# Gate and up of two feed-forwards by Strassen's scheme, in rounds, with two of four weight sums by accumulating DMAs

## The reference

```python
def swiglu(x, w_gate, w_up, w_down):
    return (jax.nn.silu(x @ w_gate) * (x @ w_up)) @ w_down
...
        h = h + 0.5 * swiglu(rms_norm(h, ffn1_norm[l]), ffn1_w_gate[l], ffn1_w_up[l], ffn1_w_down[l])
        u = rms_norm(h, mix_norm[l])
        z = u @ w_in[l]
...
        merged = jax.nn.sigmoid(ga) * (ya @ w_branch_a[l]) + jax.nn.sigmoid(gb) * (yb @ w_branch_b[l])
        h = h + merged @ w_out[l]
        h = h + 0.5 * swiglu(rms_norm(h, ffn2_norm[l]), ffn2_w_gate[l], ffn2_w_up[l], ffn2_w_down[l])
    return rms_norm(h, final_norm)
```

## Time and profile before

| | us |
|---|---|
| runs of the kernel | 1712.38, 1714.38, 1716.47 |
| median | 1714.38 |
| profiled execution, span | 1712.4 |
| TensorE busy in it | 1690.3 |
| VectorE busy | 817.3 |
| ScalarE busy | 614.4 |
| GpSimd busy | 140.8 |

### The profile page before, as it was taken

How to read it: one execution, slowest core, us unless ns; L and a number is a source line. 1 busy time by engine, 2 the same in 40 slices (tenths; PEclk the granted TensorE clock), 3 DMA queues, 4 the chain that set the end, 5 groups by cost and what they waited for, 6 DMA issues and landing times.

```text
span 1712.4 us, 22979 instructions
## 1 busy us (share of the span) xinstructions
PE 1690.3 (99%) x8175; PEld 1369.3 (80%) x8175; DVE 817.3 (48%) x1277; ACT 614.4 (36%) x1066; POOL 140.8 (8%) x149
## 2 busy tenths in 40 slices
PE   7999999999999999999999999999999999999998
PEld 5777688888888887888888887777888888888888
DVE  4888755443333344444444325765555444444332
ACT  3565644222223233222222222655543322223222
POOL 0120210000001140000001131011001100000000
PEclk9999999999999999999999999999999999999999
DMA  9743134433342334333343346122233333333332
GB/s 326 244 130 112 43 93 123 147 107 92 95 116 85 101 103 130 98 98 98 97 119 97 92 133 117 50 63 70 77 95 99 94 93 96 98 98 111 102 95 73
DMA packets 298929, 184.60 MB, mean 108 GB/s; under 512 B 14555, under 2 KB 285335, under 8 KB 298855
## 3 DMA queue, kind: packets, MB, share of 16 engines
q1 hardware_dynamic: 294112, 169.89, 33.1%
q0 software_dynamic: 4400, 13.82, 3.4%
q10 hardware_dynamic: 360, 0.13, 0.0%
HBM read 180.67 MB, written 6.36 MB: 109 GB/s over the span
## 4 chain that ended last, share of the span: by engine, by line
PE 93%; DVE 3%; ACT 2%; DMA 1%; issue 1%; DVEq 0%; ACTq 0%; SPq 0%
PE psum L567 29%; PE psum L569 28%; PE psum L568 28%; PE psum L996 1%; PE psum L961 1%; PE psum L773 1%; PE psum L1016 1%; PE psum L733 1%; DMA w_raw<-in_ffn_w_gate 1%; PE psum L749 1%; DVE w_lo L1641 1%; DVE p L1794 0%; ACT p L1289 0%; PE psum L654 0%; DMA ident<-in_k_ident 0%
## 5 line engine op out<-in xcount | busy, mean ns | idle before, releaser
L567 PE MATMUL psum<-h_hi,w_hi 128*128 128x512 f32 x1480 | 586.4, 396 | 4.6 <-DVE w_lo L1641 2.8
L569 PE MATMUL psum<-h_hi,w_lo 128*128 128x512 f32 x1480 | 576.7, 390 | 0.0
L568 PE MATMUL psum<-h_lo,w_hi 128*128 128x512 f32 x1480 | 576.6, 390 | 0.0
L1641 DVE TENSOR_TENSOR w_lo<-w_raw,w_hi 128x1024 fp32r<-128x1024 f32 (+2 forms) x266 | 348.6, 1311 | 305.0 <-ACT w_hi L1229 301.2
L1229 ACT ACTIVATE w_hi<-w_raw 128x1024 fp32r<-128x1024 f32 (+2 forms) x266 | 288.2, 1084 | 165.0 <-PE psum L569 153.4
L567 PEld LDWEIGHTS psum<-h_hi,w_hi 128*128 128x128 f32 x1480 | 277.9, 188 | 85.3 <-issue 23.9
L569 PEld LDWEIGHTS psum<-h_hi,w_lo 128*128 128x128 f32 x1480 | 277.9, 188 | 59.3
L568 PEld LDWEIGHTS psum<-h_lo,w_hi 128*128 128x128 f32 x1480 | 278.1, 188 | 55.9 <-issue 1.0
L567 PE MATMUL psum<-hid_hi,w_hi 128*128 128x512 f32 (+1 forms) x550 | 209.6, 381 | 0.0
L569 PE MATMUL psum<-hid_hi,w_lo 128*128 128x512 f32 (+1 forms) x550 | 209.3, 381 | 0.0
L568 PE MATMUL psum<-hid_lo,w_hi 128*128 128x512 f32 (+1 forms) x550 | 209.3, 381 | 0.0
(11 more groups left out here) (266 smaller groups left out, 1383.5 us busy)
## 6 DMA issues: line engine op xcount, KB each, us to landing
w_raw<-in_w_in SPq DMA_DIRECT2D x50, 512.0 KB, 3.7
w_raw<-in_w_gate_up SPq DMA_DIRECT2D x44, 512.0 KB, 3.7
w_raw<-in_ffn_w_gate SPq DMA_DIRECT2D x44, 512.0 KB, 3.7
w_raw<-in_ffn_w_up SPq DMA_DIRECT2D x44, 512.0 KB, 3.6
w_raw<-in_ffn_w_down SPq DMA_DIRECT2D x32, 704.0 KB, 4.5
w_raw<-in_w_down SPq DMA_DIRECT2D x16, 704.0 KB, 4.5
sq<-in_w_ada SPq DMA_DIRECT2D x20, 512.0 KB, 4.9
ada_w<-in_w_ada SPq DMA_DIRECT2D x16, 512.0 KB, 10.9
```

The costliest lines, as they stand in the source:

```text
L567: pe.matmul(o, a_hi, b_hi, start=start, stop=False)
L568: pe.matmul(o, a_hi, b_lo, start=False, stop=False)
L569: return pe.matmul(o, a_lo, b_hi, start=False, stop=stop)
L1641: dve.tensor_tensor(w_lo[:, s % 2, 0:n], w_raw[:, s % 2, 0:n], w_hi[:, s % 2, 0:n].bitcast(F32), ALU.subtract).then_inc(w_ready, 1)
```

## The change

For gate and up of feed-forwards 1 and 2 the product of a 2 x 2 block matrix is done with 7 block products in place of 8 (Winograd's form of Strassen's scheme). The input is cut into token halves (256) and halves of K (512 channels); the weights into gate and up, and the same halves of K. A unit is 256 columns of gate and the same of up: two hidden tiles. 11 units make up a feed-forward.

- **Inputs.** 7 blocks, A11, A12, A22 and the combinations R1 to R4, each with 4 x 256 elements per partition, high (`hq_hi`) and low (`hq_lo`). VectorE makes the combinations per channel block in `combos` (L2359) as the down or output product before it is finished; for channel blocks 0 to 3 that is one subtraction and a split of 512 elements, for 4 to 7 three operations and a split of 1280.
- **Weights.** Raw blocks in 2 sets of 5 buffers: B11 and B21 are the gate's halves of K, B12 and B22 the up's. T1 = gate half 1 added to the B12 buffer, T3 = up half 2 added to a second copy of up half 1: both by GpSimd DMAs that accumulate at their destination (`add_weights`). T2 = T1 + B22 and T4 = T2 + B21 are additions of VectorE (L2187), in place, behind the split of what they overwrite. Split weights go through a ring of 4 slots (`ring_hi`, `ring_lo`; `high` on ScalarE, `lower` L2179 on VectorE), which also serves the down projections.
- **Products** of a unit, in TensorE's order (3 x 8 matmuls of 256 tokens each): B11 into bank Y; T1 into Z; T2 onto Y; half of B21 into X; T3 onto Y; the other half of B21; T4 onto Y; B22 onto Z. In between Y holds sums that others must read first: ScalarE copies them from PSUM (`s1` before the T2 product, `u2` before T3's, `u3` before T4's), and VectorE's `first_gate` (X + s1, L2276), `second_gate` (L2285), `first_up` (Z - u2, L2294) and `second_up` (Z - u3, L2268) make gate and up of both token halves.
- **Rounds.** Units 0 to 3, 4 to 6 and 7 to 10; behind each a partial down projection over its hidden tiles, added to the residual. All three feed-forwards have these rounds; feed-forward 0 keeps its plain gate and up products. The feed-forwards' loops are unrolled.
- **out2** and feed-forward 0's last round run over channel blocks in the order `PAIRED`: 0, 4, 1, 5, and so on.
- At the second mixer's entry its first slab's split now stands behind the last block's `h_hi` and squares.

The diff, cut to its core, indented less (`f_prod` counts finished products, `prod[...]` is a product's number in it):

```diff
+TQ = T // 2
+KQ = KD // 2
+KU = KF // 2
+ROUNDS = [(0, 4), (4, 7), (7, KU)]
+KR = 2 * max(b - a for a, b in ROUNDS)
+PAIRED = [0, 4, 1, 5, 2, 6, 3, 7]
...
+hq_hi = place("hq_hi", [P, 7, KQ, TQ], F32R, HQ_AT)
+hq_lo = place("hq_lo", [P, 7, KQ, TQ], F32R, OVER)
+A11, R3, A12, A22, R1, R2, R4 = range(7)
...
+        for n, name in enumerate(("B11", "B12", "B12+", "B22", "B21")):
+            load_at((name, f, u), set_, n)
+        for name in ("P1", "Q5", "P6", "P2a", "P7", "P2", "Q4", "Q3"):
+            finish_at((name, f, u))
+        for name, n, done_ in (("B11", 0, "P1"), ("T1", 1, "Q5"), ("T2", 1, "P6"), ("T3", 2, "P7"),
+                               ("B21", 4, "P2"), ("T4", 1, "Q4"), ("B22", 3, "Q3")):
+            split_at((name, f, u), slot_no % 4, (set_, n), (done_, f, u))
+            slot_no += 1
...
+            plan(("Y", f, u), 3 * (u % 2), (f_prod, prod["Q4", f, u]), (gate_set[1], m))
+            plan(("X", f, u), 3 * (u % 2) + 1, (f_prod, prod["P2", f, u]), (c11_set, m))
+            plan(("Z", f, u), 3 * (u % 2) + 2, (f_prod, prod["Q3", f, u]), (c12_set, m))
...
+    if f == 0 and r == 0:
+        plan(("mod", GT2 // KD), 4)
...
+        plan(("down", f, r, n), 6 + i % 2, (f_prod, prod["down", f, r, n]), read)
...
+def downs(f, r, between=None):
+    ks, order = range(2 * ROUNDS[r][0], 2 * ROUNDS[r][1]), downs_of(f, r)
+    down_part(f, r, order[0], ks[:-2], True)
+    down_part(f, r, order[1], ks[:-2])
+    down_part(f, r, order[0], ks[-2:], True)
+    down_part(f, r, order[1], ks[-2:])
+    if between is not None:
+        between()
...
+def product(bank_, item, q, f, u, tiles=(0, 1), first=False, ready=None):
+    slot = in_ring[ring[item, f, u]][1]
+    hi, lo = (v[slot].rearrange("p (k n) -> p k n", n=2 * P) for v in (ring_hi, ring_lo))
+    steps = [(k, t) for k in range(KQ) for t in tiles] if ready else [(k, t) for t in tiles for k in range(KQ)]
+    fresh = first
+    for k, t in steps:
+        if ready and t == tiles[0]:
+            pe.wait_ge(q_ready, ready + 2 * k)
+        o = psum[:, bank_, TQ * t:TQ * t + TQ]
+        a_hi, a_lo = hi[:, k, P * t:P * t + P], lo[:, k, P * t:P * t + P]
+        b_hi, b_lo = hq_hi[:, q, k, :], hq_lo[:, q, k, :]
+        pe.matmul(o, a_hi, b_hi, start=fresh, stop=False, skip_group_check=True)
+        fresh = False
+        pe.matmul(o, a_hi, b_lo, start=False, stop=False, skip_group_check=True)
+        last = pe.matmul(o, a_lo, b_hi, start=False, stop=True, skip_group_check=True)
+    return last
...
+def unit(f, u, sums, spreads):
+    m = pair_count[f, u]
+    q0 = 8 * PAIR_GEN[f"ffn{f}"] if u == 0 else None
+    await_item(("B11", f, u))
+    y = take(("Y", f, u))
+    product(y, "B11", A11, f, u, first=True, ready=None if q0 is None else q0 + 1).then_inc(f_prod, 1)
+    await_item(("T1", f, u))
+    z = take(("Z", f, u))
+    product(z, "T1", R1, f, u, first=True, ready=None if q0 is None else q0 + 2).then_inc(f_prod, 1)
+    if u == 0:
+        sums()
+    await_item(("T2", f, u))
+    pe.wait_ge(s1_set, m)
+    product(y, "T2", R2, f, u).then_inc(f_prod, 1)
+    await_item(("B21", f, u))
+    x_ = take(("X", f, u))
+    product(x_, "B21", A12, f, u, (0,), first=True).then_inc(f_prod, 1)
+    pe.wait_ge(u2_set, m)
+    product(y, "T3", R3, f, u).then_inc(f_prod, 1)
+    product(x_, "B21", A12, f, u, (1,)).then_inc(f_prod, 1)
+    if u == 0:
+        spreads()
+    await_item(("T4", f, u))
+    pe.wait_ge(u3_set, m)
+    product(y, "T4", A22, f, u).then_inc(f_prod, 1)
+    await_item(("B22", f, u))
+    pe.wait_ge(c22_set, m)
+    product(z, "B22", R4, f, u).then_inc(f_prod, 1)
...
+def high(r):
+    key, slot, s_, b = in_ring[r]
+    if key[0] in ("T1", "T3"):
+        act.wait_ge(sum_landed[s_][key[0] == "T3"], 16 * sums_count[key[1:]][1])
+    elif key[0] in ("T2", "T4"):
+        act.wait_ge(f_added, 2 * pair_count[key[1:]] - (key[0] == "T2"))
+    else:
+        act.wait_ge(part_landed[s_][b], 16 * raw_count[key])
+    if ring_free[key] is not None:
+        act.wait_ge(f_prod, prod[ring_free[key]])
+    n = D if key[0] != "down" else 2 * P * len(units_of(key[2]))
+    act.activation(ring_hi[slot][:, 0:n], pool_raw[s_][b][:, 0:n], ACT.Identity).then_inc(f_high, 1)
...
+def unit(f, u, r, scales):
+    m, first, last = pair_count[f, u], u == ROUNDS[r][0], u == ROUNDS[r][1] - 1
+    k = 2 * (u - ROUNDS[r][0])
+    y = bank["Y", f, u]
+    act.wait_ge(f_prod, prod["P1", f, u])
+    if m > 1:
+        act.wait_ge(c11_set, m - 1)
+    if u == 0:
+        act.wait_ge(summed, SUM0 + SQUARES["down0" if f == 1 else "out2"] + KD * (2 if f == 1 else 1))
+    act.activation(s1, psum[:, y, :], ACT.Copy).then_inc(s1_set, 1)
+    high_after("B11", f, u)
+    if not first:
+        silu(f, u - 1, 0)
+    high_after("T1", f, u)
+    if not first:
+        silu(f, u - 1, 1)
+    act.wait_ge(f_prod, prod["P6", f, u])
+    if m > 1:
+        act.wait_ge(c12_set, m - 1)
+    act.activation(u2, psum[:, y, :], ACT.Copy).then_inc(u2_set, 1)
+    high_after("T2", f, u)
+    if not first:
+        for h in (1, 0):
+            hidden_high(f, u - 1, h, k - 2)
+    if u == 0:
+        scales()
+    act.wait_ge(f_prod, prod["P7", f, u])
+    if m > 1:
+        act.wait_ge(c22_set, m - 1)
+    act.activation(u3, psum[:, y, :], ACT.Copy).then_inc(u3_set, 1)
...
+for i, n in enumerate(PAIRED):
+    wait_summed("out2", i, None)
+    if i < KD - 1:
+        split_high(S_OUT2 + i + 1)
+    if i >= KQ:
+        high(FIRST_ITEM[2] + i - KQ)
+    wait_new("out2", i, None, 1)
+    take_h(i, n, "ffn2", col_of("ffn2_norm_2", n, None, 1))
+    act.activation(sq[:, i % 2, 0, :], x[:, n, :], ACT.Square).then_inc(squared, 1)
+    parts_high(n, "ffn2")
...
+def lower(r):
+    key, slot, s_, b = in_ring[r]
+    dve.wait_ge(f_high, r + 1)
+    if r - FIRST_ITEM[2 if key[1] == 2 else 0] == 3:
+        dve.wait_ge(w_used, S_OUT2 + KD if key[1] == 2 else S_OUT1 + KD)
+    n = D if key[0] != "down" else 2 * P * len(units_of(key[2]))
+    raw_ = pool_raw[s_][b]
+    dve.tensor_tensor(ring_lo[slot][:, 0:n], raw_[:, 0:n], ring_hi[slot][:, 0:n].bitcast(F32),
+                      ALU.subtract).then_inc(f_ready, 1)
+    if key[0] in ("T1", "T2"):
+        f, u = key[1:]
+        other = ("B22" if key[0] == "T1" else "B21", f, u)
+        o_set, o_b = raw_home[other]
+        dve.wait_ge(part_landed[o_set][o_b], 16 * raw_count[other])
+        dve.wait_ge(f_ready, r + 1)
+        dve.tensor_tensor(raw_[:, :], raw_[:, :], pool_raw[o_set][o_b][:, :], ALU.add).then_inc(f_added, 1)
...
+def unit(f, u, r, scale_cols, scales):
+    first, last = u == ROUNDS[r][0], u == ROUNDS[r][1] - 1
+    k = 2 * (u - ROUNDS[r][0])
+    low_after("B11", f, u)
+    if not first:
+        second_gate(f, u - 1)
+    low_after("T1", f, u)
+    if not first:
+        first_up(f, u - 1)
+        hidden(f, u - 1, 1)
+    low_after("T2", f, u)
+    if not first:
+        hidden(f, u - 1, 0)
+        for h in (1, 0):
+            hidden_low(f, u - 1, h, k - 2)
+    if u == 0:
+        scale_cols()
+    low_after("T3", f, u)
+    second_up(f, u)
+    low_after("B21", f, u)
+    if last:
+        first_gate(f, u)
+    low_after("T4", f, u)
+    if u == 0:
+        scales()
+    if last:
+        second_gate(f, u)
+    low_after("B22", f, u)
+    if last:
+        first_up(f, u)
+        for h in (0, 1):
+            hidden(f, u, h)
+        for h in (0, 1):
+            hidden_low(f, u, h, k)
+    else:
+        first_gate(f, u)
...
+def combos(n, name):
+    gen, pair = 8 * PAIR_GEN[name], 2 * (n % KQ)
+    dve.wait_ge(h_taken, gen + pair + n // KQ + 1)
+    def part(dst, a, b, op):
+        return dve.tensor_tensor(h_parts[:, dst, :], h_parts[:, a, :], h_parts[:, b, :], op)
+    if n < KQ:
+        part(H3, H11, H21, ALU.subtract).then_inc(combos_set, 1)
+        dst, src, high_ = hq_lo[:, A11:R3 + 1, n % KQ, :], h_parts[:, H11:H3 + 1:2, :], hq_hi[:, A11:R3 + 1, n % KQ, :]
+    else:
+        done(part(H1, H21, H22, ALU.subtract))
+        done(part(H2, H1, H11, ALU.subtract))
+        part(H4, H12, H2, ALU.add).then_inc(combos_set, 1)
+        dst, src, high_ = hq_lo[:, A12:R4 + 1, n % KQ, :], h_parts[:, H12:H4 + 1, :], hq_hi[:, A12:R4 + 1, n % KQ, :]
+    dve.wait_ge(q_high, gen + pair + n // KQ + 1)
+    dve.tensor_tensor(dst, src, high_.bitcast(F32), ALU.subtract).then_inc(q_ready, 1)
...
+def add_weights(f, u, w_gate, w_up):
+    set_, nth = sums_count[f, u]
+    gate, up = (w.rearrange("(k p) n -> p k n", p=P) for w in (w_gate, w_up))
+    cols = slice(2 * P * u, 2 * P * u + 2 * P)
+    for n, (key, src) in enumerate((("B12", gate[:, 0:KQ, cols]), ("B12+", up[:, KQ:KD, cols]))):
+        s_, b = raw_home[key, f, u]
+        pool.wait_ge(part_landed[s_][b], 16 * raw_count[key, f, u])
+        dst = pool_raw[s_][b][:, :].rearrange("p (k n) -> p k n", n=2 * P)
+        pool.dma_start(dst, src, accum_op=ALU.add).then_inc(sum_landed[s_][n], 16)
...
-pool.wait_ge(hid_ready, 2 * KF)
+for u in range(1, KU):
+    add_weights(1, u, *weights1)
```

(1 more changed line is left out.)

719 lines of the change are left out of this document (465 added, 254 removed).

## The result

The changed kernel takes 1741.63 us (1739.57 to 1743.54), the kernel before beside it 1715.15: the ratio is 1.0157, 95% interval 1.0141 to 1.0172. The forecast was 1717 with a range of 1702 to 1736, so the time lies 5.6 us above the range and the slowdown of 26 us is ten times the 2.5 us worked out. A second measurement (`a0_changed_again`) gave 1741.12, ratio 1.0168.

The account below looks back on a forecast made before the run. TensorE was taken to bound the kernel, busy 1690 of 1712.4 us. Terms -35.8 + 12.8 + 8.7 + 6.3 + 5.7 + 3.0 + 1.8 = +2.5 us gave 1714.9 profiled, forecast 1717 us, range 1702 to 1736.

Parts of the forecast that it names:

- Matmuls: Gate and up of both feed-forwards: 2112 matmuls of 512 columns become 3696 of 256, -35.8 us.
- Rival (d): Weight loads run in series with matmuls, 0.213 us per matmul: 2061 us; chance 0.01.
- u2: In 16 units with a predecessor, TensorE waits 0.8 us for ScalarE's copy before T3's product: +12.8 us.
- Rival (b): VectorE's chain with slower handoffs sets a longer period per unit: 1733 us at 0.1 us each; chance 0.27.
- Entry: Second mixer's first matmul waits for its first slab's split, now behind the last block's work: +5.7 us.
- Output projection: Second mixer's output projection: combinations ahead of the next weight split make TensorE wait, +8.7 us (6 to 11).
- starts: Starts of the second and third feed-forwards: TensorE waits for the last block's combinations, +6.3 us (4 to 9).
- GpSimd's queue: Second feed-forward's unit 1: accumulating transfers stand behind 16 near_rows transfers, +3.0 us (0 to 6).
- rival (c): Accumulating DMAs are slow, deciding when two take over 21 us; at 25 us, 1797 us; chance 0.07.
- Small ones: Ends of 3-unit rounds +1.0, first feed-forward's third down product +1.4, last block's steps -0.6: +1.8 us.
- Low clock: TensorE's granted clock: the prediction had no term for it, counted as 0.

Follow-up runs that it names:

- Experiment 5: Changed kernel with GpSimd adding only 16 of 512 columns of the squares in both feed-forward inputs and after the down projections: 1722.42 us, ratio 1.0053.
- experiment 2: Changed kernel with the second mixer's first slab split ahead of the last channel block's residual, h_hi, squares and h_lo: 1736.2 us, ratio 1.0131.
- experiment 3: Changed kernel with the output projection's weight split for the product after next ahead of the block's combinations in ScalarE's and VectorE's queues: 1742.43 us, ratio 1.0173.
- v2_direct_sums: Changed kernel with six reordering moves, TensorE instead of GpSimd summing the last two blocks' squares, and one ScalarE wait moved: 1705.7 us, ratio 0.9958.
- e1_sums_first: Experiment 1: changed kernel with GpSimd issuing unit 1's two accumulating transfers of feed-forward 1 ahead of the 16 near_rows transfers: 1734.25 us, ratio 1.0134.

## Why the prediction was wrong, step by step

- **Matmuls (-35.8): right.** A 256-column matmul starts every 0.12 us (707.11, 707.23, 707.35 in the changed kernel), as the earlier trace rows said. Rival (d), weight loads in series, is out, and with it the Trainium skill's rule as I read it, that a load overlaps running matmuls only when the row group differs (TensorE: Matmul & The Clock Gate, "The mechanism").
- **u2 (+12.8): the mechanism right, the size off.** The chain ran as walked. VectorE ended T3's split 3.8 us into the unit, ScalarE began s1 at 4.5, but the operations behind that followed each other more closely than I took them (0.60 us for a 512 one behind another, where I took 0.73). The end of the chain, and TensorE's matmul behind it:

```profile
706.83 0.69 DVE L2294 TENSOR_TENSOR c<-psum,sq 128x512 f32<-128x512 f32 x1
...
707.61 0.60 ACT L1724 ACTIVATE sq<-psum 128x512 f32<-128x512 f32 x1 [1.16 <-DVE c L2294]
...
708.26 0.39 PE L1038 MATMUL psum<-hq_hi,ring_hi 128*128 128x256 f32 x1
```

  The stall is 0.3 to 0.5 us, not 0.8, 16 times: 6.0 us. Rival (b), slower handoffs, is out.
- **Entry (+5.7): right**, 5.6, except for the low clock behind it.
- **Output projection (+8.7), starts (+6.3): sums near, causes incomplete.** Together they came to 19.0, where I had 15.0. I had priced GpSimd's additions at 0.3 us per block, though the earlier trace rows showed a split at 2.34 instead of 1.23, and the earlier trace rows one at 1.66 where I took 1.1. (The product of the earlier trace rows is the last of out2, and 1338.72 begins feed-forward 2, not a product of out2; the price of the chain is the same at each.) Experiment 5 shows that they made 10 us of these two terms, and the 2.7 us in feed-forward 0's last round that I had at nothing. I hadn't followed SP's queue either, where the change puts five loads in front of the projection's fourth slab. In the changed kernel that slab landed in time; in the profiles of experiments 2 and 3 it did not.
- **GpSimd's queue (+3.0): mis-sized**, 8.0. The start of near_rows, the 7.7 us behind it and the slower landing were each taken too short. Here rival (c) has a part: accumulating transfers are slower (8.2 to 10.3 us against 5.9 to 6.1), which matters at one unit, not at all of them.
- **Small ones (+1.8): mis-sized**, 10.1. The wait at the end of a 4-unit round is 0.7 us where I had none, and of a 3-unit round 1.7 where I had 0.5; six rounds make 6.1. I had walked the hidden tile's chain without the weight splits that stand in it.
- **Low clock (0): the step that is missing.** I priced each stall at its own length. The six stalls of 3.3 to 6.0 us from feed-forward 1 on each had low clock beside or behind them, and none of 2.6 us or less had. Length alone doesn't decide it: in `v2_direct_sums` the clock fell behind a stall of 2.1 us, and behind one-column matmuls without a stall; in `e1_sums_first` it held behind one of 3.6 us, at the place where 3.3 us had lowered it in the changed kernel. What decides between such cases isn't shown. The earlier trace rows stated the clock, and I did not ask what a stall would do to it. It is the largest single error, 11.5 us, and alone more than the distance to the range.

The rest of the difference is the sum of 5.0 (queue), 8.3 (small), 4.0 (projection and starts), less 5.9 (u2). The range held the unknown price of the handoffs, but not that the boundary terms could all err in the same direction, as terms do that share an engine.

## What to carry to other kernels

Fewer products don't pay at the boundaries: here 36 us of matmul time were saved, and 61 given back where stages meet, by work put into queues that had been just full. Walk every queue past which a step moves, DMA queues too, and price a stall of TensorE at its length plus the low clock behind it, which a busy share doesn't show. Where two engines work beside each other, take the stretched duration that the trace has, not the lone one.

## What the runs showed of the hardware

- TensorE's granted clock fell to 0.50 at stalls of 3.3 to 6.0 us and cost 1.5 to 2.9 us each in the matmuls of 256 and 512 columns; with 36 transposes in such a stall it stayed at 1.00. It also fell behind one-column matmuls that kept TensorE busy (`v2_direct_sums`, 643.8), and it held behind one stall of 3.6 us (`e1_sums_first`, 1327).
- Three 256-wide additions of VectorE took 1.4 us alone and 2.3 to 3.4 us beside GpSimd's 512-wide ones.
- An accumulating DMA of 512 KB from GpSimd's queue landed 8.2 to 10.3 us after its issue, a plain one of the same size in the same place 5.9 to 6.1.
- Behind the 16 transfers near_rows GpSimd issued nothing for 7.7 us in the changed kernel, and for 10.3 in that of experiment 1; with plain transfers it issued one more and then paused for 7.1. The next issue came 0.3 us (0.5 with plain transfers) behind the landing of the last of the 16. Whether it waits for that landing wasn't tested.
